# Sample attention of a hybrid decoder step: first output chunk ahead of the scores, output rows ahead of the next weights' parts, third slab sooner

## The reference

```python
h = rmsnorm(x, norm1_g) * (1 + scale1) + shift1            # shift, scale, gate from silu(c) @ w_ada
qa, ka, va, qb, kb, vb, r, log_a = project(h, w_in, ...)   # one projection, 6160 columns
oa = mix_a(qa, ka, va)    # 16 heads of 64, three (window, dilation) branches, merged
ob, gla_state = mix_b(qb, kb, vb, log_a)                   # 4 GLA heads, dk 128, dv 256
x = x + gate1 * (concat(rmsnorm(oa), rmsnorm(ob) * silu(r)) @ w_out)
h2 = rmsnorm(x, norm2_g) * (1 + scale2) + shift2
x = x + gate2 * ((silu(conv(h2 @ w_up_gate)) * (h2 @ w_up)) @ w_down)
```

## Time and profile before

| | |
|---|---|
| time, median of 3 runs | 1542.83 us (1542.47 to 1544.98) |
| profiled execution | span 1544.0 us, 27862 instructions |
| PE busy | 1514.8 us (98%) |
| PEld busy (weight loads, beside PE) | 1372.8 us (89%) |
| DVE busy | 875.7 us (57%) |
| ACT busy | 633.9 us (41%) |
| POOL busy | 52.4 us (3%) |
| DMA | 370.98 MB, mean 240 GB/s |
| mean granted TensorE clock | 0.993 |

### The profile page before, as it was taken

One profiled execution on the slowest core, in us unless ns is written; L12 is line 12 of the kernel. 1 busy time (PEld: TensorE's weight loads), 2 busy tenths in 40 slices (PEclk: granted clock), 3 DMA queues, 4 the chain that ended last, 5 costly groups with the idle time before them and its releaser, 6 DMA issues.

```text
span 1544.0 us, 27862 instructions
## 1 busy us (share of the span) xinstructions
PE 1514.8 (98%) x11762; PEld 1372.8 (89%) x11762; DVE 875.7 (57%) x1509; ACT 633.9 (41%) x873; POOL 52.4 (3%) x89
## 2 busy tenths in 40 slices
PE   8999999999999889999999999999999999999999
PEld 4877888888888557768899999999999999999999
DVE  3655676666667435557454555555554565656574
ACT  3433444434445215235333333334333445545453
POOL 2000000001111000000000000000000000000000
PEclk8999999999999999999999999999999999999999
DMA  9998777777777997997644444454545444454541
GB/s 354 400 355 346 307 257 257 257 259 267 255 288 270 413 414 309 422 363 292 251 164 164 164 164 169 159 184 147 188 146 182 163 172 178 166 181 172 178 176 53
DMA packets 62283, 370.98 MB, mean 240 GB/s; under 512 B 7431, under 2 KB 7913, under 8 KB 27081
## 3 DMA queue, kind: packets, MB, share of 16 engines
q1 hardware_dynamic: 56096, 351.08, 60.6%
q0 software_dynamic: 5904, 17.93, 3.4%
q10 hardware_dynamic: 162, 0.22, 0.0%
HBM read 359.32 MB, written 9.88 MB: 239 GB/s over the span
## 4 chain that ended last, share of the span: by engine, by line
PE 89%; DMA 5%; DVE 3%; SPq 2%; ACT 1%; issue 1%; POOL 0%; ACTq 0%; DVEq 0%
PE ps L989 26%; PE ps L990 25%; PE ps L991 25%; PE ps L941 4%; PE ps L934 1%; SPq L710 1%; DMA ring<-in_w_ada_early 1%; DMA ring<-in_w_out 1%; DMA ring<-in_cache_k_win 1%; DMA proj<-in_tables 1%; ACT whi L1501 1%; DVE wlo L2028 1%; PE ps L1321 1%; DMA ring<-in_w_ada 1%; PE ps L1290 1%
## 5 line engine op out<-in xcount | busy, mean ns | idle before, releaser
L989 PE MATMUL ps<-hhi,whi 128*128 128x288 f32 x3136 | 934.0, 298 | 3.1 <-DVE wlo L1871 1.6
L990 PE MATMUL ps<-hlo,whi 128*128 128x288 f32 x3136 | 922.6, 294 | 0.0
L991 PE MATMUL ps<-hhi,wlo 128*128 128x288 f32 x3136 | 922.5, 294 | 0.0
L989 PEld LDWEIGHTS ps<-hhi,whi 128*128 128x128 f32 x3136 | 589.0, 188 | 38.8 <-issue 29.9
L990 PEld LDWEIGHTS ps<-hlo,whi 128*128 128x128 f32 x3136 | 589.2, 188 | 0.7
L991 PEld LDWEIGHTS ps<-hhi,wlo 128*128 128x128 f32 x3136 | 588.9, 188 | 0.0
L1492 ACT ACTIVATE whi<-ring 128x1024 fp32r<-128x1024 f32 x178 | 185.7, 1060 | 200.7 <-PE ps L991 200.7
L1864 DVE TENSOR_TENSOR wlo<-ring,whi 128x1024 fp32r<-128x1024 f32 x178 | 212.0, 1221 | 78.8 <-ACT whi L1492 78.4
L2028 DVE TENSOR_TENSOR wlo<-ring,whi 128x1024 fp32r<-128x1024 f32 x96 | 117.0, 1223 | 79.6 <-ACT whi L1501 79.5
L1501 ACT ACTIVATE whi<-ring 128x1024 fp32r<-128x1024 f32 x96 | 100.8, 1053 | 130.1 <-PE ps L991 114.2
L2545 DVE TENSOR_TENSOR wlo<-ring,whi 128x1024 fp32r<-128x1024 f32 (+1 forms) x94 | 105.7, 1132 | 56.2 <-ACT whi L1805 56.2
(11 more groups left out here) (298 smaller groups left out, 905.4 us busy)
## 6 DMA issues: line engine op xcount, KB each, us to landing
ring<-in_w_up SPq DMA_DIRECT2D x88, 1024.0 KB, 4.8
ring<-in_w_down SPq DMA_DIRECT2D x32, 1408.0 KB, 6.1
ring<-in_w_ada SPq DMA_DIRECT2D x42, 1024.0 KB, 6.8
ring<-in_w_in SPq DMA_DIRECT2D x28, 1024.0 KB, 6.5
ring<-in_w_ada_early SPq DMA_DIRECT2D x22, 1024.0 KB, 7.5
proj<-in_w_ada SPq DMA_DIRECT2D x22, 1024.0 KB, 11.0
ring<-in_w_in_early SPq DMA_DIRECT2D x20, 1024.0 KB, 9.3
ring<-in_w_out SPq DMA_DIRECT2D x16, 1024.0 KB, 13.2
```

Of the source, the lines that this page charges most:

```text
L989: mm(out, w_hi, x_hi, start=start, stop=False)
L990: mm(out, w_hi, x_lo, start=False, stop=False)
L991: return mm(out, w_lo, x_hi, start=False, stop=stop)
```

## The change

Three edits to the written-out order. Nothing is added or taken away on any engine.

- TensorE: in groups 1 to 3, `out_product(3g)` stands ahead of the group's scores, not behind them.
- ScalarE and VectorE: in each group, `output(g)` stands ahead of the parts of chunk 3g+4, not behind them. On VectorE `output(g)` waits for the turn on TensorE, on ScalarE for the end of `values(g)`.
- SyncE: slab 2 (`out_half(2)`, chunks 4 and 5) is asked for ahead of cache units 30 and 31.

```diff
--- before.py
+++ after.py
@@ -723,8 +723,9 @@
             cache_load(8)
             out_half(0)
             out_half(1)
-            cache_loads(9, 32)
+            cache_loads(9, 30)
             out_half(2)
+            cache_loads(30, 32)
             out_half(3)
             cache_loads(32, 52)
             out_half(4)
@@ -1340,6 +1341,8 @@
                 last.then_inc(*OT.step(f"sums{n}"))
 
             for g in range(NB // 2):
+                if g:
+                    out_product(3 * g)
                 scores(g, 8)
                 scores(g, 9)
                 new_scores(g)
@@ -1347,8 +1350,6 @@
                     if n == 4 and g:
                         output(g - 1)
                     scores(g, n)
-                if g:
-                    out_product(3 * g)
                 out_product(3 * g + 1)
                 probabilities(g)
                 out_product(3 * g + 2)
@@ -1702,8 +1703,8 @@
                 out_hi(3 * g + 2)
                 probabilities(g)
                 out_hi(3 * g + 3)
+                output(g)
                 out_hi(3 * g + 4)
-                output(g)
             act.wait_ge(*SU.upto("out", 3))
             for n in range(2):
                 f(proj[:, 8 + 4 * n:12 + 4 * n, :], proj[:, 4 * n:4 * n + 4, :], ACT.Square).then_inc(*OA.step(f"sq{n}"))
```

## The result

| | before | changed |
|---|---|---|
| time, median (lowest to highest), 11 runs each | 1543.62 us (1542.44 to 1545.90) | 1547.46 us (1546.34 to 1549.73) |
| ratio to before, 95% interval | | 1.0028 (1.0020 to 1.0036) |
| span of the profiled execution | 1544.0 us | 1547.9 us |

The changed kernel is slower, by 3.8 us by the medians and 4.3 us by the ratio. The prediction had 1544.8 us with a range to 1546.8. Its likeliest case named the right place and the right size of the wait there; what it left out of its sum, the lower clock behind that wait, came on top in the profiled execution.

A forecast was written before the change was run, and what follows sets the result against it. It took the cache-unit stream to bound the stage from about 495 us. -0.95 at values(3) and +2.4 before chunk 13 give +1.45, or +2.4 without the gain; taken as +2.0: 1544.8 us, range 1542.6 to 1546.8.

The forecast's parts named there:

- likeliest case: Whole kernel: the prediction's own forecast of 1544.8 us, own range 1543.6 to 1545.8, chance 0.55.
- The stream bounds the stage: Sample attention from about 495 us: the stream of cache units, not TensorE, times the last value unit, landing at 591.3.
- The sign that the prediction named: Group 3's last value tile released by a DMA would show the forecast right; no size given.
- The third slab at 518.4: SyncE's stream: slab issued two units sooner lands at about 518.4, not 520.97; worth nothing at the end.
- The lead at the end of values(1): Group 1 on TensorE: values(1) starts 4.3 us sooner and ends at 537.8; the gain doesn't last.
- The sixth slab at about 546.9: SyncE issues `out_half(5)` at about 546.9 instead of 539.2, behind chunk 7's low parts, with no hole in the stream.
- the rival of the dry stream: At the sixth slab the queue empties: +4.3 us, 1547.1 us, chance 0.07.
- The fit for a lone transfer: One DMA takes about 2.0 us fixed plus bytes over 436 GB/s, 4.4 us for 1 MB.
- its margin: Time to spare at the sixth slab: 2.0 us with a lone slab of 4.8 us, 2.3 by the skill's rule.
- A gain of 0.95 us at values(3): End of group 3: values(3) ends at 593.2 instead of 594.12, held by the unit landing at 591.3.
- The wait before chunk 13: After group 3's turn, TensorE waits for VectorE's copy and low parts: 2.78 less 0.36, cost 2.4 us.
- the clock case: At chunk 13 and the head sums, the clock falls behind the new wait: 1.3 us more, about 1546.1, chance 0.22.

The follow-up runs named there:

- rows first in groups 0 to 2: Kernel before, with output rows ahead of the next parts on ScalarE and VectorE in groups 0 to 2 only: 1543.69 us, ratio 0.9999.
- group 3 undone: Changed kernel, but in group 3 ScalarE and VectorE make chunk 13's parts ahead of the output rows again: 1544.04 us, ratio 1.0008.
- the filled waits: Changed kernel with nine or five idle products on TensorE between group 3's turn and chunk 13: 1550.91 us and 1546.35 us.
- group 3 alone changed: Kernel before, with output rows ahead of chunk 13's parts on ScalarE and VectorE in group 3 only: 1547.19 us, ratio 1.0027.
- nine products: Changed kernel with nine idle 128x256 matmuls on TensorE between group 3's turn and chunk 13: 1550.91 us (5 runs), ratio 1.0047.

## Why the prediction was wrong, step by step

- **The stream bounds the stage: right in the main.** Removing 5.09 us of waiting (rows first in groups 0 to 2) moved the time by nothing that can be told. Values(3) ended at 592.61 to 593.97 us with TensorE's edit alone (592.61), with rows first in groups 0 to 2 (592.84), with group 3 undone (593.71) and in the changed kernel (593.97). The sign that the prediction named, a last value tile released by a DMA, is in the first three and not in the changed kernel's profile, where the lower clock had made TensorE late.
- **The third slab at 518.4, chunk 4 at 523.4, chunk 5 at about 529.1, chunk 8 at 553.5: right.** They came at 518.07, 523.78, 529.46 and 553.22. The waits of about 0.3, 0.4 and 1.1 to 1.4 us around single chunks are there as 0.36, 0.27 and 1.11 to 1.38. The lead at the end of values(1) is 3.9 us, where 4.3 was forecast.
- **The sixth slab at about 546.9 without a hole: right,** 547.51; the rival of the dry stream fell. The fit for a lone transfer that the prediction takes from the Trainium skill is given there for DMAs issued by GpSimd, while the slabs here are issued by SyncE. The lone slab of rows 3 took 4.8 us, 0.4 more than the 4.4 us of that fit. The queue did not run dry at the sixth slab, so what such a stop would cost was not measured. (By the prediction's own numbers its margin is 2.4 us and not 2.3.)
- **A gain of 0.95 us at values(3): not there.** In the profiled execution the clock fell at 584.0 over chunk 11 and used up its lead, so values(3) ended at 593.97 and not at 593.2. The prediction had allowed for that gain being nought, for another reason (runs whose old path had no fall at 577), and split the difference at +2.0. The full +2.4 fits the measurement better.
- **The wait before chunk 13, +2.4 us: right in place and size,** 2.46 us from turn to chunk. It is gone when VectorE's edit is undone.
- **The step that failed** is the cost of the lower clock behind the new wait. It stood under the rivals with a chance of 0.22, and the sum of the forecast had it at nothing. In the profiled execution the wait of 2.22 us is followed by 1.6 us of lower clock (the rival had 1.3): 2.46 + 1.6 is 4.1 us, where the medians are 3.8 apart. Five idle products that keep TensorE at work in the wait take 1.1 to 1.7 us off. The size in a usual execution is less sure. The changed kernel lies 3.1 us (ratios) to 3.3 us (medians) above the one with group 3 undone, and 2.46 of that is the wait, which leaves 0.6 to 0.8 us. Of the two profiles that have the wait unfilled, the clock fell behind it in one. So the wait is shown as the cause of some 2.5 us. That the clock behind it costs more is supported by the filled waits; how often it falls there, and so how much of the remaining 1.4 us of the medians is its doing, stays open.
- **The base** was low: the median of before over 11 runs is 1543.62, not the 1542.83 of the three that were given. The forecast is 2.66 us off. Of that 0.8 is the base, 0.46 the wait (2.46 against the +2.0 taken), and 1.4 what the sum left out. That a range to 1546.8 "holds nearly all of the clock case" was wrong too: with the base and the wait as measured, that case lies above it.
- **The profiled execution of before** was further from the median than I took it to be. In all runs listed the time is the span and 1.5 to 1.6 us more (1549.49 for a span of 1547.9), so the span of 1544.0 stood for some 1545.6, 2 us over the median. Its clock is lower from 522.1, where the 5.09 us wait ends, from 576.8 and from 686.0 (the stretch at 577 is in rows 1):

```profile
522.10:525.60 3.50, 3.03 (x24) 1.69 (x28) 2.04 (x9) 0.41 (x1) 0.00 (x0) 0.52 1.02 413
...
686.00:689.30 3.30, 3.30 (x17) 0.73 (x10) 2.36 (x2) 1.08 (x2) 0.00 (x0) 0.50 0.54 151
```

The profile of the kernel with group 3 undone has none of the three.

## What to carry to other kernels

Where a transfer stream runs without a gap, as here, the waits before its last unit can be worth nothing, even one of 5 us. Look at what stands between its last unit and the next long stretch: in this stage that was the part with a price. An edit applied to all turns of a loop has to be checked at the last turn by itself: there the consumer came right behind the producer, and the cover of the other turns was missing. And a new wait of some 2 us on TensorE is to be priced with the lower clock that may follow it, here 1.6 us in the execution where it did.

## What the runs showed that I had not expected

- Waits far shorter than the 5.09 us one are followed by a lower clock, and not each time that the same wait stands there: behind the 2.22 us wait at 600 in the changed kernel's profile and not in that of the kernel with group 3 alone changed; at 686 behind a wait of 1.76 us (684.47, the row below) in the kernel before, and not in the kernel with group 3 undone, whose profile has the same wait and a span of 1541.9 us.
- An idle product of 128x256 in plain float32 takes 0.41 us, three times the 0.13 us of a 288-column product of the split parts.
- With nine products the clock stayed up at chunk 13 and fell at 632, behind the longer wait there. The products had not done away with a fall, and the kernel was the slowest of all.

```profile
684.47 1.24 PE L928 MATMUL ps<-work,con 128*128 128x288 f32 x4 [1.76 <-DVE work L1916]
```
